# ConvFFN up product of a streaming encoder layer: two plain slab pairs instead of three, and another order of the vector and scalar work around the first recursive pair

## The reference, cut to what matters

```python
def conv_ffn(h, conv_past, w_up, conv_w, conv_b, w_down):      # h: (tokens, 1024)
    u, g = jnp.split(jnp.einsum('btd,df->btf', h, w_up), 2, axis=-1)   # w_up: (1024, 2 * 2816)
    u_ext = jnp.concatenate([conv_past.astype(u.dtype), u], axis=1)
    c = conv_b + u_ext[:, 0:t] * conv_w[0]
    for i in range(1, CONV_W):                                  # CONV_W = 3
        c = c + u_ext[:, i:i + t] * conv_w[i]
    y = jax.nn.gelu(c, approximate=True) * g
    return jnp.einsum('btf,fd->btd', y, w_down), u_ext[:, -(CONV_W - 1):]
```

## Time and profile before

| | |
|---|---|
| time, 3 runs | 1558.34, 1559.72, 1562.19 us (median 1559.72) |
| the profiled execution | 1557.92 us, of which the profile's span is 1556.1 us |
| PE busy | 1498.4 us, 96% of the span |
| DVE, POOL, ACT busy | 1033.4, 615.3, 601.3 us |
| mean granted TensorE clock | 0.993 |
| chain that ended last | PE 79%, DVE 9%, DMA 3%, POOL 3% |

### The profile page before, as it was taken

One profiled execution on the slowest core, in us unless ns is written; L12 is line 12 of the kernel. 1 busy time (PEld: TensorE's weight loads), 2 busy tenths in 40 slices (PEclk: granted clock), 3 DMA queues, 4 the chain that ended last, 5 costly groups with the idle time before them and its releaser, 6 DMA issues.

```text
span 1556.1 us, 25737 instructions
## 1 busy us (share of the span) xinstructions
PE 1498.4 (96%) x9803; PEld 1400.5 (90%) x9803; DVE 1033.4 (66%) x2024; ACT 601.3 (39%) x1250; POOL 615.3 (40%) x405
## 2 busy tenths in 40 slices
PE   6999999999999999999999999999999999999996
PEld 5899999999997989889887999999999999778885
DVE  6876667767674359876444996655555555578986
ACT  5133534435342235655323333333333332444463
POOL 6522232222222332125231568878888782000104
PEclk9999999999999999999999999999999999999999
DMA  6232222222132730118531112222222228723568
GB/s 198 68 89 69 74 91 65 68 73 71 30 96 75 235 105 24 56 56 286 179 116 58 45 59 93 83 83 78 75 80 67 74 83 280 236 98 115 170 196 153
DMA packets 156474, 165.40 MB, mean 106 GB/s; under 512 B 14005, under 2 KB 121913, under 8 KB 156353
## 3 DMA queue, kind: packets, MB, share of 16 engines
q1 hardware_dynamic: 119689, 109.34, 22.5%
q10 hardware_dynamic: 34840, 51.14, 9.9%
q0 software_dynamic: 1824, 3.28, 1.5%
HBM read 125.56 MB, written 39.85 MB: 106 GB/s over the span
## 4 chain that ended last, share of the span: by engine, by line
PE 79%; DVE 9%; DMA 3%; POOL 3%; ACT 2%; issue 2%; ACTq 1%; SPq 1%; DVEq 0%; POOLq 0%
PE bank L1106 16%; PE bank L1108 16%; PE bank L1107 16%; PE bank L1112 6%; PE bank L1114 6%; PE bank L1113 6%; PE bank L1138 4%; PE bank L1247 2%; PE bank L1218 1%; PE bank L1217 1%; DVE rowsn L2360 1%; POOL ring_l L1048 1%; DVE kl L2381 1%; PE bank L1594 1%; PE bank L1596 1%
## 5 line engine op out<-in xcount | busy, mean ns | idle before, releaser
L951 POOL TENSOR_TENSOR ring_h<-raw,att 128x1024 fp32r<-128x1024 f32 x48 | 98.8, 2058 | 507.4 <-PE bank L1108 499.1
L1106 PE MATMUL bank<-ht_h,ring_h 128*128 128x352 f32 x816 | 268.7, 329 | 2.0 <-POOL ring_l L952 1.4
L1108 PE MATMUL bank<-ht_h,ring_l 128*128 128x352 f32 x816 | 263.1, 322 | 0.0
L1107 PE MATMUL bank<-ht_l,ring_h 128*128 128x352 f32 x816 | 262.5, 322 | 0.0
L1106 PE MATMUL bank<-m_h,ring_h 128*128 128x264 f32 x648 | 184.2, 284 | 1.2 <-DVE m_l L2854 1.2
L1107 PE MATMUL bank<-m_l,ring_h 128*128 128x264 f32 x648 | 184.2, 284 | 0.0
L1108 PE MATMUL bank<-m_h,ring_l 128*128 128x264 f32 x648 | 183.9, 284 | 0.0
L1106 PEld LDWEIGHTS bank<-ht_h,ring_h 128*128 128x128 f32 x816 | 153.7, 188 | 5.5 <-issue 2.0
L1107 PEld LDWEIGHTS bank<-ht_l,ring_h 128*128 128x128 f32 x816 | 154.4, 189 | 0.7
L1108 PEld LDWEIGHTS bank<-ht_h,ring_l 128*128 128x128 f32 x816 | 153.9, 189 | 0.0
L952 POOL TENSOR_TENSOR ring_l<-raw,ring_h 128x1024 fp32r<-128x1024 f32 x48 | 129.8, 2703 | 3.8
(11 more groups left out here) (380 smaller groups left out, 3836.9 us busy)
## 6 DMA issues: line engine op xcount, KB each, us to landing
raw<-in_w_up SPq DMA_DIRECT2D x44, 512.0 KB, 3.9
raw<-in_w_in SPq DMA_DIRECT2D x34, 512.0 KB, 3.9
rb<-in_w_down SPq DMA_DIRECT2D x66, 256.0 KB, 2.9
d_y<-conv SPq DMA_DIRECT2D x22, 529.0 KB, 3.2
d_gate<-gst ACTq DMA_DIRECT2D x48, 176.0 KB, 1.9
a<-d_y SPq DMA_DIRECT2D x33, 256.0 KB, 5.7
ra<-d_y SPq DMA_DIRECT2D x33, 256.0 KB, 2.7
gm<-d_gate ACTq DMA_DIRECT2D x8, 528.0 KB, 4.4
```

The source lines that it names most:

```text
L951: order.link(nc.gpsimd.tensor_tensor(high, src, zero.to_broadcast(list(src.shape)), ALU.add))
L1106: nc.tensor.matmul(out, wh, xh, start=start, stop=False, skip_group_check=onto)
L1107: nc.tensor.matmul(out, wh, xl, start=False, stop=False, skip_group_check=onto)
L1108: return nc.tensor.matmul(out, wl, xh, start=False, stop=stop, skip_group_check=onto)
```

## The change

`PLAIN` goes from 3 to 2: pair 2 becomes the first recursive pair. With one pair less ahead of it, the work that prepares the recursive pairs is arranged anew:

- DVE makes all four token sums and their low parts without anything in between; the convolution and gating of pairs 0 and 1, which stood among them, go into pair 2 and pair 3.
- The high part of plain slabs of pair 1 is made by ACT (`plain_high`), and POOL only makes the low part; two POOL splits (pair 2's) are gone.
- The seven weight blocks lie in other ring places (`SLOT`).
- In pair 2 ACT does `c11_out` and gelu(0) between the first and the second weight block of pair 3, and gelu(1) after the last.
- The store of y(0) stands behind both loads of pair 3, that of y(1) behind both loads of pair 4.

```diff
--- before.py
+++ after.py
@@ -68,7 +68,8 @@
 
 HB = TOK // 2
 CB = HB // 2
-PLAIN = 3
+PLAIN = 2
+SLOT = dict(P1=2, P6=3, P2=4, P7=5, P5=0, P4=1, P3=6)
 PRODUCTS = ["P1", "P6", "P2", "P7", "P5", "P4", "P3"]
 PLAIN_ORDER = [("u", 0, 0), ("u", 0, 1), ("v", 0, 0), ("v", 0, 1), ("u", 1, 0), ("v", 1, 0), ("u", 1, 1), ("v", 1, 1)]
 GAP = 2
@@ -300,7 +301,7 @@
 
     def ring_part(lo, name):
 
-        return (o_rl if lo else o_rh) + BLOCK * dict(P1=0, P2=1, P6=2, P4=3, P7=4, P5=5)[name]
+        return (o_rl if lo else o_rh) + BLOCK * SLOT[name]
 
     o_tb = [R1 + 32 * HB * i for i in range(3)]
     o_raw_u = o_raw + 4 * D * (S_FFN % NRAW)
@@ -430,6 +431,7 @@
     up_full = sem("up_full")
     up_act = sem("up_act")
     up_dve = sem("up_dve")
+    plain_highs = sem("plain_highs")
     w_high = sem("w_high")
     w_ready = sem("w_ready")
     sums_made = sem("sums_made")
@@ -884,13 +886,13 @@
             for f in range(PLAIN - 1):
                 up_load(f + 2, 0)
                 up_load(f + 2, 1)
-            for f in range(PLAIN - 1):
-                y_store(f)
             for f in range(PLAIN - 1, FT - 2):
                 for j in range(2):
                     up_load(f + 2, j)
-                    if j == 0 and f >= PLAIN:
+                    if j == 0 and f > PLAIN:
                         y_store(f - 1)
+                if f <= PLAIN:
+                    y_store(f - PLAIN + 1)
             y_store(FT - 3)
             for i, load in enumerate(LOADS):
                 if i == 2 * HK:
@@ -935,7 +937,7 @@
 
         def slot(name):
 
-            i = dict(P1=0, P2=1, P6=2, P4=3, P7=4, P5=5, P3=6)[name]
+            i = SLOT[name]
             if i == 6:
                 return ws_h[:, :, :], ws_l[:, :, :]
             return tuple(w[:, i // 2, 4 * (i % 2):4 * (i % 2) + 4, :] for w in (ring_h, ring_l))
@@ -1021,13 +1023,9 @@
 
                 for j in range(2):
                     n = S_FFN + 2 * f + j
-                    pool.wait_ge(raw_in[n % NRAW], 16 * (n // NRAW + 1))
-                    if n - NSPL >= S_FFN:
-                        g, i = divmod(n - NSPL - S_FFN, 2)
-                        pool.wait_ge(up_full, plain_done(g, (6, 7)[i]))
-                    else:
-                        pool.wait_ge(chunk_full, CHUNKS)
-                    ring_split(n)
+                    pool.wait_ge(plain_highs, 2 * (f - 1) + j + 1)
+                    nc.gpsimd.tensor_tensor(flat(ring_l[:, n % NSPL]), flat(raw[:, n % NRAW]),
+                                            flat(ring_h[:, n % NSPL]).bitcast(F32), ALU.subtract).then_inc(slab_split, 1)
 
             def weight_sums(f):
 
@@ -2076,12 +2074,22 @@
                 if f > PLAIN:
                     act.wait_ge(up_full, product_done(f - 1, name, 1))
                 else:
-                    act.wait_ge(up_full, dict(P1=plain_done(PLAIN - 2, 7), P2=plain_done(PLAIN - 2, 7),
-                                              P6=plain_done(PLAIN - 1, 6), P4=plain_done(PLAIN - 1, 6),
-                                              P7=plain_done(PLAIN - 1, 7), P5=plain_done(PLAIN - 1, 7),
+                    act.wait_ge(up_full, dict(P1=plain_done(PLAIN - 2, 7), P6=plain_done(PLAIN - 2, 7),
+                                              P2=plain_done(PLAIN - 1, 6), P7=plain_done(PLAIN - 1, 6),
+                                              P5=plain_done(PLAIN - 1, 7), P4=plain_done(PLAIN - 1, 7),
                                               P3=plain_done(PLAIN - 1, 7))[name])
                 h, _, x = weight_block(f, name)
                 copy(h, x).then_inc(w_high, 1)
+
+            def plain_high(i):
+
+                n = S_FFN + 2 + i
+                act.wait_ge(raw_in[n % NRAW], 16 * (n // NRAW + 1))
+                if i:
+                    act.wait_ge(up_full, plain_done(0, 6))
+                else:
+                    act.wait_ge(chunk_full, CHUNKS)
+                copy(ring_h[:, n % NSPL], raw[:, n % NRAW]).then_inc(plain_highs, 1)
 
             def token_high(i):
 
@@ -2169,43 +2177,51 @@
             for f in range(PLAIN):
                 for i in range(len(PLAIN_ORDER)):
                     plain_evict(f, i)
+                    if f == 0 and i == 2:
+                        plain_high(0)
                     if f == 0 and i == 3:
                         mix_high(NT)
-                    if f == 1 and i == 1:
+                    if f == 0 and i == 6:
+                        plain_high(1)
+                    if f == 1 and i == 2:
                         token_high(2)
-                    if f == 1 and i == 3:
-                        gelu(0)
+                    if f == 1 and i == 4:
+                        weight_high(PLAIN, "P1")
+                        weight_high(PLAIN, "P6")
                     if f == 1 and i == 5:
                         token_high(0)
-                    if f == 2 and i == 1:
+                    if f == 1 and i == 7:
+                        weight_high(PLAIN, "P2")
                         token_high(3)
-                    if f == 2 and i == 3:
-                        gelu(1)
-                    if f == PLAIN - 1 and i == 4:
-                        weight_high(PLAIN, "P1")
-                    if f == PLAIN - 1 and i == 6:
-                        weight_high(PLAIN, "P6")
-                        weight_high(PLAIN, "P2")
-                    if f == PLAIN - 1 and i == 7:
-                        for name in PRODUCTS[3:]:
-                            weight_high(PLAIN, name)
+                        weight_high(PLAIN, "P7")
             for f in range(PLAIN, FT):
                 more = f + 1 < FT
                 p1_out(f, 0)
                 p1_out(f, 1)
                 if f == PLAIN:
                     token_high(1)
+                    for name in PRODUCTS[4:]:
+                        weight_high(f, name)
                 if more:
                     weight_high(f + 1, "P1")
+                if f == PLAIN:
+                    c11_out(f, 0)
+                    c11_out(f, 1)
+                    gelu(0)
+                if more:
                     weight_high(f + 1, "P6")
-                c11_out(f, 0)
-                c11_out(f, 1)
+                if f > PLAIN:
+                    c11_out(f, 0)
+                    c11_out(f, 1)
                 if more:
                     weight_high(f + 1, "P2")
-                gelu(f - 1)
+                if f > PLAIN:
+                    gelu(f - 1)
                 if more:
                     for name in PRODUCTS[3:]:
                         weight_high(f + 1, name)
+                if f == PLAIN:
+                    gelu(f - 1)
             operand_highs(0)
             operand_highs(1)
             sample_high(0)
@@ -2932,28 +2948,28 @@
 
             first_tokens()
             last_tokens()
-            conv_taps(0, (0, 1, 2))
             token_low(2)
+            other_tokens()
             token_low(0)
-            other_tokens()
-            gated(0)
-            conv_taps(1, (0, 1, 2))
             token_low(3)
-            gated(1)
+            token_low(1)
             for f in range(PLAIN, FT):
-                conv_taps(f - 1, (0, 1))
+                if f > PLAIN:
+                    conv_taps(f - 1, (0, 1))
                 u_sum(f, "u2", 0)
                 u_sum(f, "u2", 1)
-                conv_taps(f - 1, (2,))
-                if f == PLAIN:
-                    token_low(1)
+                conv_taps(*((0, (0, 1, 2)) if f == PLAIN else (f - 1, (2,))))
                 u_sum(f, "u3", 0)
                 u_sum(f, "u3", 1)
+                if f <= PLAIN + 1:
+                    gated(f - PLAIN)
+                    dve.wait_ge(y_done, f - PLAIN + 1)
                 out_sum(f, "c22", 0)
                 out_sum(f, "c22", 1)
                 if f + 1 == FT:
                     operand_lows(0)
-                gated(f - 1)
+                if f > PLAIN:
+                    gated(f - 1)
                 if f + 1 == FT:
                     operand_lows(1)
                     sample_low(0)
@@ -2964,6 +2980,8 @@
                     operand_lows(3)
                 out_sum(f, "c12", 0)
                 out_sum(f, "c12", 1)
+                if f == PLAIN:
+                    conv_taps(f - 1, (0, 1, 2))
             conv_taps(FT - 1, (0, 1, 2))
             gated(FT - 1)
```

## The result

The changed kernel takes 1566.94 us in the median of 9 runs (1563.1 to 1568.54), the kernel before, beside it, 1558.79 us (1557.72 to 1563.85, 9 runs). The ratio is 1.0039, with a 95% interval of 1.0029 to 1.0049. The forecast was 1566.9 us. The profiled execution took 1567.32 us, of which 1565.5 us are the span.

A forecast was written before the change was run, and what follows sets the result against it. PE, busy 96% of the span, was taken as the bound: 1557.9 - 2.9 - 1.9 + 9.5 + 2.5 = 1565.1 us profiled, 1566.9 us as the median of runs. The range, to hold 8 in 10, was 1561.5 to 1570 us.

The forecast's parts named there:

- The removed work: Up stage: 24 matmuls less (-2.9 us) and the old waits gone (-1.9 us), 4.8 us at most.
- the old waits: Transition into the recursive pairs in the kernel before: PE loses 1.9 us, mostly one gap ahead of P5; removed, -1.9 us.
- The four waits: PE's new waits at P7, P4 and P3 of pair 2 and P2 of pair 3: +9.5 us in sum.
- P7: Pair 2: this product waits 1.2 us for u2 on DVE, bounds 0 to 3.7.
- P4: Pair 2: this product waits 1.9 us for u3, which stands behind conv_taps(0) on DVE.
- P3: Pair 2: this product waits 2.5 us for c22, behind convolution, c11_out, table load, gelu(0) and gated(0).
- P2: Pair 3: this product waits 3.9 us for p1_out, which stands behind conv_taps(1) and gelu(1).
- Turns of DVE and POOL: Transition: each waits for the other's instruction to end; a turn costs about 1.15 us, convolutions take 7.2 to 7.6 us.
- The rival without turns: Transition: POOL is not in DVE's way; waits 1.0 us, no slow clock, 1555.9 us; chance 0.09.
- The clock: PE at half clock after P2's wait once, after P3's in some two of three cases: +2.5 us (0 to 3.4).
- The table load: Ahead of gelu(0): 1.28 us; rival: ACT held longer by a drain, 0.5 us at most, 1567.4 us, chance 0.03.
- The backlog goes on into pair 3: Rival: in pair 3 gated(1), gated(2) and conv_taps(2) use up the slack; +2 us, 1568.9 us; chance 0.12.

The follow-up runs named there:

- e10: The kernel before, with the first convolution tap of the first two plain pairs on ACT instead of DVE; 1559.09 us, ratio 0.9989.
- e4: The changed kernel, with POOL computing only 8 of 512 columns of the low parts of pairs 2 and 3, except P3's; 1565.38 us, ratio 1.0029.
- e2: The changed kernel, with a one-element gelu on ACT late in pair 0 so the table load happens there; 1567.22 us, ratio 1.0042.
- e1: The changed kernel, with gelu(1) behind both p1_out copies of pair 3 on ACT instead of ahead of them; 1566.14 us, ratio 1.0040.
- e6: The changed kernel with three shifts: gelu(1) behind p1_out, table load early, token_high(2) one evict earlier; 1565.93 us, ratio 1.0034.
- e9: The changed kernel without shifts, with the first convolution tap of both plain pairs on ACT instead of DVE; 1563.22 us, ratio 1.0016.
- e8: e6 plus two more shifts in the second recursive pair, and the first convolution tap of both plain pairs on ACT; 1559.58 us, ratio 0.9993.

## Why the prediction was right

**The removed work.** 24 matmuls and the old waits, 4.8 us (4.7 by the starts): right, and e10 shows that the old waits were of the same kind, since 2 us less of DVE's work takes all of them away.

**The four waits.** Place and releaser of each were right, and the sum too, 9.0 for 9.5. P7 1.45 for 1.2, P4 1.89 for 1.9, P3 2.07 for 2.5, P2 3.57 for 3.9. P3 was less since gated(0) took 1.79 us and not 2.12. The convolutions took 7.2 and 7.4 us, for 7.2 to 7.6. P7 was put together rightly as well: DVE starts the first low part at 889.77, 35.5 us into the stage, as worked out (886.6 less 851.1), and from there to u2 it takes 21.8 us, for 16.5 + 5.0. Only its upper bound does not follow: seven turns of 1.15 us give a wait of 4.3 us and not 3.7.

**Turns of DVE and POOL.** Right, and shown by e4, which gives the taps of the first convolution their durations back without touching them. The rival without turns would have needed convolutions near 4 us.

**The clock.** The term was mis-sized, +2.5 for 1.5. Behind the gap of 3.57 us the stretch came once, as put; the "two of three cases ahead of P3" did not. Behind idle times of 1.7 to 1.9 us the clock stayed at 1.00 in the up stage of every kernel here, though in the attention stage it falls after 1.91.

**The table load.** Its rival is out. The gelu starts 0.02 us behind the load's record (920.20 + 1.28, then 921.50), and e2 won 1.2 us at P3 by moving it. The Trainium skill, "ScalarE: Activation LUTs", section "What ACT_TABLE_LOAD costs", has 2.66 us for a switch, drain included; the trace agrees with its load of about 1.28 us, and neither place shows the drain.

**The backlog goes on into pair 3**: not in the changed kernel, which waits nowhere behind P2. But it is there: e1 takes P2's wait away, and it stands at P7 of the pair instead. What I did not see is that the four waits are in large part one. The prediction worked out each from its own chain and was right by that, since each chain passes through the same late DVE. Read as four causes it would have promised e6 a gain of 5 us or more; its stage was 1.0 shorter, 2.2 less in waits and 1.2 more in clock.

**The total.** That 1566.94 meets 1566.9 is in part luck. The forecast starts from a median of 1559.72, and the kernel before, timed beside the changed one, has 1558.79, so the measured change is 8.2 us, where I had 7.2. The terms make +5.8 in the stage; the other 2.3 us by which the medians differ lie outside the stage, where nothing that the runs show ties them to the change.

## What to carry to other kernels

When several waits follow each other in a transition, add up the work of the engines that they wait for, before giving each wait a cause: if moving one thing makes the next step wait, it is a backlog. Shifts win little of it (e6: 2.2 of 9.0 us of waits); less work shortens it, or work on an engine with room, here 3.0 us on ACT in place of 5.0 on DVE in its turns. Work of the engine that bounds the kernel can be the cover of the others': taking 2.9 us off PE cost 7 us of waits here, and taking 2.5 off it in the old order gained 0.3. Relieve the covered engines first, and then see what the shorter order is worth: with the relief, the longer order needed no wait at all; the shorter one was 4 us slower with the same relief (e9), and only level with it after five shifts more (e8).
